# A hybrid attention and mixture-of-experts step: gate sums of the first head pair loaded during the last projection, and the attention step's turns and norms in another order

## The reference

```
sc = (einsum('bqhd,bkhd->bhqk', qi, k) * SCALE + ci[..., None] - c_k[:, :, None, :])
sc = where(kpos <= qpos, sc, -inf)
pr = softmax(sc, axis=-1)
return einsum('bhqk,bkhd->bqhd', pr, v)
```

## Time and profile before

| | us |
|---|---|
| median of 3 executions | 977.05 (973.55 to 977.14) |
| the profiled execution | 977.28 |
| its span, first to last instruction | 975.5 |
| its mean granted TensorE clock | 0.934 of full |
| TensorE matmul busy | 826.5 (85%) |
| VectorE busy | 476.0 (49%) |
| ScalarE busy | 334.0 (34%) |

### The profile page before, as it was taken

How to read it: one execution, slowest core, us unless ns; L and a number is a source line. 1 busy time by engine, 2 the same in 40 slices (tenths; PEclk the granted TensorE clock), 3 DMA queues, 4 the chain that set the end, 5 groups by cost and what they waited for, 6 DMA issues and landing times.

```text
span 975.5 us, 16424 instructions
## 1 busy us (share of the span) xinstructions
PE 826.5 (85%) x5956; PEld 720.9 (74%) x5956; DVE 476.0 (49%) x1219; ACT 334.0 (34%) x854; POOL 89.0 (9%) x148
## 2 busy tenths in 40 slices
PE   4999999999747888897999699999469999999700
PEld 3999999999726776776989588888356777777500
DVE  4731111101126666666878636555518444444368
ACT  5631111110126566563656533322112222222223
POOL 0000000000000000000000000000123433343200
PEclk9999999999859999999999799999669999999955
DMA  8301114111051602005000412211789999982196
GB/s 260 101 20 44 44 43 134 43 43 52 17 149 55 56 15 51 1 2 217 2 1 0 169 49 87 87 44 54 273 299 325 339 323 329 336 318 97 56 348 222
DMA packets 62493, 124.53 MB, mean 128 GB/s; under 512 B 13387, under 2 KB 34723, under 8 KB 62435
## 3 DMA queue, kind: packets, MB, share of 16 engines
q1 hardware_dynamic: 53219, 105.91, 32.3%
q0 software_dynamic: 9216, 17.85, 5.1%
HBM read 108.72 MB, written 30.73 MB: 143 GB/s over the span
## 4 chain that ended last, share of the span: by engine, by line
PE 74%; DVE 12%; DMA 6%; ACT 4%; issue 3%; SPq 0%; DVEq 0%; POOLq 0%; ACTq 0%; POOL 0%
PE ps L1503 33%; PE ps L1843 11%; PE ps L1849 5%; PE ps L1612 3%; PE ps L1596 3%; PE ps L1836 3%; PE ps L1689 3%; PE ps L1722 2%; DVE big L1105 2%; DMA work<-c_rows 2%; PE ps L1627 2%; PE ps L1782 2%; PE ps L1554 1%; ACT big L758 1%; PE ps L1706 1%
## 5 line engine op out<-in xcount | busy, mean ns | idle before, releaser
L1503 PE MATMUL ps<-wg_hi,xl 128*128 128x256 f32 x576 | 163.4, 284 | 0.2 <-DVE wg_lo L991 0.2
L1503 PE MATMUL ps<-wg_hi,xh 128*128 128x256 f32 x576 | 163.0, 283 | 0.0
L1503 PE MATMUL ps<-wg_lo,xh 128*128 128x256 f32 x576 | 163.0, 283 | 0.0
L1503 PEld LDWEIGHTS ps<-wg_hi,xl 128*128 128x128 f32 x576 | 110.6, 192 | 0.4 <-issue 0.4
L1503 PEld LDWEIGHTS ps<-wg_lo,xh 128*128 128x128 f32 x576 | 110.6, 192 | 0.0
L1503 PEld LDWEIGHTS ps<-wg_hi,xh 128*128 128x128 f32 x576 | 110.6, 192 | 0.0
L1843 PEld LDWEIGHTS ps<-fox,work 128*128 128x128 f32 x320 | 60.6, 190 | 19.4 <-issue 12.2
L1843 PE MATMUL ps<-fox,work 128*128 128x256 f32 x320 | 72.5, 379 | 2.0 <-DVE work L1401 2.0
L1612 PE MATMUL ps<-cf,big 128*128 128x128 f32 x312 | 49.5, 286 | 23.5 <-ACT big L758 21.5
L1401 DVE COPY work<-ps 128x512 f32<-128x512 f32 x32 | 22.1, 691 | 95.6 <-PE ps L1836 95.5
L758 ACT ACTIVATE big<-big,nm 128x384 f32<-128x384 f32 (+7 forms) x72 | 53.9, 751 | 25.4 <-DVE nm L1105 25.0
(11 more groups left out here) (285 smaller groups left out, 1776.8 us busy)
## 6 DMA issues: line engine op xcount, KB each, us to landing
fox<-in_w_gate SPq DMA_DIRECT2D x20, 512.0 KB, 4.7
fox<-in_w_up SPq DMA_DIRECT2D x20, 512.0 KB, 6.7
fox<-in_w_down SPq DMA_DIRECT2D x20, 512.0 KB, 6.7
work<-in_w_in SPq DMA_DIRECT2D x8, 1024.0 KB, 5.5
fox<-y_rows SPq DMA_DIRECT2D x16, 512.0 KB, 6.8
h_rows<-big SPq DMA_DIRECT2D x9, 512.0 KB, 2.6
work<-in_x_prompt SPq DMA_DIRECT2D x8, 512.0 KB, 4.7
fox<-in_w_out SPq DMA_DIRECT2D x1, 4096.0 KB, 12.8
```

Source lines behind the costliest of these rows:

```text
L1503: mm = pe.matmul(out, xs[a](c), ws[b](c), start=(c + k == 0), stop=(c == C - 1 and k == 2))
```

## The change

The buffer layout of `work` is another: `cB[0]` takes columns 0 to 2815, `ck` 2816 to 3839, `cv` 3840 to 4863. `cB[0]` no longer shares columns with the ninth group's weights; `cv` now does. SP issues `load_c(0)` right after the store of the gate sums has landed, ahead of its wait for the whole projection, and `cv` behind that wait. TensorE's wait for the caches goes from ahead of the attention to the first transpose of a cached key, in step 3. In the attention's step TensorE's `fback(n-2)` goes ahead of `fturn(n, 1)`, and VectorE's `fnorm(n-2)` goes ahead of `fcopy(n, 1, 1)` and `fmax(n+1, 1)`.

```
-        ck = cut(work, 0, 2, NH * DH)
-        ck_h = rounded("ck_h", work_at, 0, 2, NH * DH)
-        cv = cut(work, 2 * NH * DH, 2, NH * DH)
-        at = 4 * NH * DH
-        cB = [[cut(work, at + u * NK * P, NK * P) for u in range(2)], [...]]
-        at += 2 * NK * P
+        at = 2 * NK * P
+        ck = cut(work, at, 2, NH * DH)
+        ck_h = rounded("ck_h", work_at, at, 2, NH * DH)
+        at += 2 * NH * DH
+        assert at <= 4 * D
+        cv = cut(work, at, 2, NH * DH)
+        cB = [[cut(work, u * NK * P, NK * P) for u in range(2)], [...]]
+        at += 2 * NH * DH
...
-            sp.dma_start(cv, t["cache_fox_v"]...).then_inc(s["cache_in"], 16)
...
             sp.wait_ge(s["c_out"], 16)
+            load_c(0)
             sp.wait_ge(s["proj_done"], NT * NG)
-            load_c(0)
+            sp.dma_start(cv, t["cache_fox_v"]...).then_inc(s["cache_in"], 16)
             load_c(1)
...
                 if n + 1 < NF:
                     fmax(n + 1, 0)
+                if n >= 2:
+                    fnorm(n - 2)
                 if halves(n) > 1:
                     fcopy(n, 1, 1, 5)
                 if n + 1 < NF:
                     fmax(n + 1, 1)
-                if n >= 2:
-                    fnorm(n - 2)
...
                 for m in range(first, end):
+                    if m == NT:
+                        pe.wait_ge(s["cache_in"], 64)
...
-            pe.wait_ge(s["cache_in"], 64)
...
                 if n + 1 < NF:
                     fqk(n + 1)
-                fturn(n, 1)
                 if n >= 2:
                     fback(n - 2)
+                fturn(n, 1)
```

More of the change, by code:

```diff
@@ L172, in build @@
         w0_lo, w0_hi = rounded("w0_lo", swa_at, 0, C, WF), rounded("w0_hi", swa_at, C * WF, C, WF)
-        ck = cut(work, 0, 2, NH * DH)
-        ck_h = rounded("ck_h", work_at, 0, 2, NH * DH)
-        cv = cut(work, 2 * NH * DH, 2, NH * DH)
-        at = 4 * NH * DH
-        cB = [[cut(work, at + u * NK * P, NK * P) for u in range(2)], [cut(fox, NT * QKV + u * NK * P, NK * P) for u in range(2)]]
-        at += 2 * NK * P
+        at = 2 * NK * P
[4 more added lines that the diff above has]
+        cv = cut(work, at, 2, NH * DH)
+        cB = [[cut(work, u * NK * P, NK * P) for u in range(2)], [cut(fox, NT * QKV + u * NK * P, NK * P) for u in range(2)]]
+        at += 2 * NH * DH
         sqst = cut(work, at, NT, P)
@@ L406, in _ @@
             sp.dma_start(ck, t["cache_fox_k"].rearrange("l b (t p) h d -> p (l b t) (h d)", p=P)).then_inc(s["cache_in"], 16)
-            sp.dma_start(cv, t["cache_fox_v"].rearrange("l b (t p) h d -> p (l b t) (h d)", p=P)).then_inc(s["cache_in"], 16)
             sp.dma_start(skv[:, 0:2 * DH], t["cache_swa_k"].rearrange("l b p h d -> p (l b h d)")).then_inc(s["cache_in"], 16)
@@ L419, in _ @@
             sp.wait_ge(s["c_out"], 16)
+            load_c(0)
             sp.wait_ge(s["proj_done"], NT * NG)
-            load_c(0)
+            sp.dma_start(cv, t["cache_fox_v"].rearrange("l b (t p) h d -> p (l b t) (h d)", p=P)).then_inc(s["cache_in"], 16)
             load_c(1)
```

## The result

The changed kernel takes 964.48 us (963.02 to 967.51, 4 runs), the kernel before, beside it, 977.1. The ratio is 0.9878, 95% interval 0.9849 to 0.9907: faster by 12.6 us, where 12.0 and 965.0 were forecast. The profiled execution took 965.73.

The account below looks back on a forecast made before the run. The prediction took the late load of the gate sums as the bound at the hand-over, then the attention's ring through three engines. It summed -15.9 + 2.1 + 1.8 = -12.0 us, from 977.05 to 965.0, range 961.5 to 968.5.

Parts of the forecast that it names:

- The stall of the gate sums: Start of the forgetting attention: the first maximum moves from 280.4 to 264.5 us, 15.9 us gained, all on the chain.
- Store and load: Gate sums' trip through device memory: store landed at 241, load of 18.9 us in at 259.9, 4.6 us before needed.
- The cached values: Key staging in step 3: their load costs nothing; 5 us if it landed with the 1.4 MB behind it.
- The clock at the hand-over: Projection to attention: TensorE's clock stays low in steps 0 to 2, so 0 gained, 2.1 us at most.
- rival 2: Start of the attention: the clock doesn't stay down and is up by step 1, giving 962.9 us; chance 0.13.
- The norm: Staged attention steps: the norm ahead of VectorE's second maximum lengthens its ring, 0.7 us in each of three pairs, 2.1 lost.
- the back turn: Twelve unstaged attention steps: ahead of TensorE's second turn it adds 0.12 us, or 0.25 in three of them, 1.8 lost.
- the staged run is 0.7 us longer: Sign expected in the new profile: the attention's staged run of tiles 5 to 8 takes some 0.7 us more.
- Rival 1: Attention: the ring over TensorE was the bound, its 10.1 us of norm waits come back, 951.0 us; chance 0.15.
- rival 3: Attention: norm and back turn cost in every step, 16.3 and 7.6 us, 985.1; chance 0.04 in full, 0.05 in part.
- Behind the attention: Stages after the forgetting attention, the sliding-window attention among them: the prediction's sum had no term for them.

Follow-up runs that it names:

- e7: The changed kernel with the cached values loaded behind the second head pair's gate sums instead of ahead of them; 970.16 us, ratio 0.9928.
- e1: The load alone: the changed kernel with VectorE's norm and TensorE's back turn in their old places; 959.29 us, ratio 0.9822.
- e5: e1 plus ten extra TensorE products with unread results, six ahead of the scores of step 0 and four behind them; 960.77 us.
- e3: e1 with the norm early and the back turn in its old place; 964.41 us.
- e4: e1 with the back turn early and the norm in its old place; 964.42 us.
- e2: The kernel before with only the new order of norm and back turn, the load still late; 980.81 us, ratio 1.0036.
- e12: e1 plus 11 extra TensorE products with unread results ahead of step 30, to delay the sliding-window attention; 964.41 us, ratio 0.9880.
- e9: The changed kernel measured again, unaltered, on the same chip as e10; 964.25 us, ratio 0.9871.
- e11: e1 with norm and back turn early only in steps 4, 5, 13, 14, 22 and 23; 961.68 us.
- e10: e1 measured again, unaltered, on the same chip as e9; 957.96 us, ratio 0.9807.

## Why the prediction was right, point by point

- **The stall of the gate sums** (15.9 us): shown, slightly undersized. The first maximum leads by 16.8 us (16.2 to 17.1 in all kernels with the early load). It follows its own scores, as forecast; these ran at the full clock, 0.4 us faster, and the projection ended 0.5 us earlier.
- **Store and load** (issue at 241, landed by 259.9, cover 4.6 us): issued at 239.5, landed by 258.2, cover 5.4 us; no kernel with the early load waits for it. The pair took 18.7 us, as in the kernel before (18.9). The 2 us that the prediction takes from the Trainium skill, "DMA: Bandwidth & Descriptors", section "Anatomy of one DMA", is given there for transfers that GpSimd issues; SP issues the load once its store is in, and that was 4.0 us after the store here.
- **The cached values** (nothing, 5 us if they land with the 1.4 MB): both ends shown. TensorE has no DMA wait in step 3, the values landed at 264.4 (266 forecast), and e7 measured 4.3 us of wait and 5.9 us of lead.
- **The clock at the hand-over** (0, at most 2.1): mis-sized. The lead grows by 1.0 us from step 0 to 4 in the changed kernel, 1.5 in e1. The clock was low for 6.8 us and 3.4 us there, in the kernel before for 10 us of steps. This is rival 2, in part. (The lower end of the range, 961.5, doesn't follow from this term: 965.0 - 2.1 is 962.9.) That the fall can be pushed away without a gain (e5) I had not seen.
- **The norm** (2.1) **and the back turn** (1.8): each alone is right, 1.9 in e3 and 1.8 in e4. The step that failed is adding them: together they cost 1.6 us (1.5 in e2), not 3.9. The changed kernel's unstaged steps lose 0.4, 0.4 and 0.65 us, as in e4, and its three staged runs 0.1 in all: the back turn's term stands, and the norm's is all but gone. The norm takes 331.20 - 330.79 = 0.41 of VectorE's ring, not 0.48, the idle 0.28 and 0.55 us absorb it at tiles 6 and 7, and with the back turn early the norm is ready sooner when its place comes: e3 waits 7.3 us there, in seven waits; without the early back turn the move costs 1.9. Up to tile 7 a staged run gains a little; at tile 8 it loses 0.39, where I said 0.5. So the sign "the staged run is 0.7 us longer" didn't come, and the lead at step 35 is 16.2 where 12 was named. Rival 1 (TensorE's 10.1 us come back) and rival 3 (a cost in every step) are ruled out by e1 and e2.
- **Behind the attention** (nothing): the missing term. The changed kernel loses 3.7 us in the sliding-window attention by two stretches of low clock, 0.6 at the stage's start and 3.0 in its middle, and its lead is 11.7 at the end. The terms in front were 4.2 us better than forecast, 16.2 instead of 12.0, and this took it back: the total is right because two errors cancel, and that is luck. e12 shows that the fall can come in the old order. Why it comes in some profiles and not in others stays open: the leads with a fall (15.6, 16.1, 17.2, 17.6 among them) and without (16.5, 17.4, 18.6) are mixed. One thing does go with it. Where step 16's pause is in its old place, the clock fell in the middle in just those profiles in which it had been low for 6.8 us in all around the stage's start (the changed kernel, e2, e3, e4, e7, e9, e11, e12), and not where that was 3.4 us (before, e1, e5, e10). So what the stage finds at its start matters as well as the pause; what sets that wasn't tested.
- **The order's full price**, 5 to 6 us against the load alone, is thus 1.6 to 2.4 us in the attention, shown by rows (0.8 of the 2.4 is e9's further fall of the clock), and the rest behind it, seen in both profiles of the changed kernel and in e2, but whose dependence on the order itself wasn't separated from that on the start.

## What to carry to other kernels

Look for a small buffer whose place makes its load wait: here moving 11 KB a partition off the weights' columns and issuing the load sooner removed 17 us, all of the change's worth. A wait that an engine shows (10.1 us for a norm) is not to be had if another ring of the same step has as little slack (0.28 to 0.55 us here, none at tile 8): take both rings' idle time before moving work from one to the other, and time each half of a change alone, since half of this one costs 5 us.

## What the runs showed of the hardware

- Eleven extra products that delayed one stage by 2.4 us cost 5 us in all (e12 against e1): the sliding-window attention's middle ran at the lower clock, 1.2 GHz, for 6.8 us and lost 3.0 us, with the same code, in some kernels, and at 2.4 GHz in others that reach it 1 to 3 us sooner or later.
- A pause of 1.59 us in that stage ended with the clock's fall in the changed kernel and in e12, and without one in e1 and e10. The stage's first stretch of low clock was 6.8 us long in the former and 3.4 in the latter.
- Ten products that keep TensorE busy over a pause kept the clock up there and had it fall 15 us later, in a pause of 1.46 us, where 1.5 us of lead went (e5).
- Executions of one kernel spread over 2.5 us (e4) to 7 us (955.3 to 962.3 for the load alone), and e1's single profile is 3.2 us off its median.
- A load of 512 KB landed 3.5 us after its issue ahead of two loads of 704 KB, and 21.9 us after it behind them (e7).
